# The first projection of a two-block kernel in four quarters of its input dimension, with the modulation weights read in smaller units around it

## The chip, the cores and the metric

The kernel runs on one core of one Trainium2 chip. The core has TensorE (matrix multiply, called PE in the profile; its weight loads are listed as PEld), VectorE (DVE), ScalarE (ACT), GpSimd (POOL) and SyncE (SP), and 16 DMA engines that bring data from HBM. The metric is device time in microseconds (us), lower is better; below, a time "at 68.65" is counted from the start of the span of the profiled execution.

## The reference

Two transformer-like blocks over 256 tokens of width 2048, all in float32. Only the first block's head matters here:

```
mod = silu(c) @ w_ada + b_ada                     # c: 1 x 2048, w_ada: 2048 x 12288 (96 MB)
sh1, sc1, gt1, sh2, sc2, gt2 = split(mod, 6)
h = rmsnorm(x, g) * (1 + sc1) + sh1
proj = h @ w_in[l]                                # 2048 x 3072: xr, gr, xp
xr = causal_dwconv(xr, w_conv, b_conv)            # 4 taps
hr = rg_lru(xr, ...)                              # two gates (small matmuls), sigmoid, exp, scan
y_pool = pool_mixer(xp, w_pool, ls_pool)          # windows of 2, 4, 8, 16, then a small matmul
y = concat(hr * gelu(gr), y_pool) @ w_out         # 2048 x 2048
x = x + gt1 * y                                   # then the FFN with sh2, sc2, gt2
```

So `sc1` and `sh1` are needed before the first product, `gt1` with the second product, the other three for the FFN. The second block has no modulation.

## The kernel before

Weights are streamed once from HBM; the activations stay in SBUF, features on the partitions and the 256 tokens along the free dimension. The weights come as **slabs** of 256 output columns, each slab in four **chunks** of 512 rows of the input dimension K (0.5 MiB each: 4 K-tiles of 128 rows). The stages up to the FFN are IN (12 slabs, 48 chunks) and OUT (8 slabs, 32 chunks).

A chunk goes through a fixed path. SP loads it into one of 8 `raw` buffers (`load`), ScalarE writes its high part (`convert`, L907, `split[..0..]`), VectorE the low part (L1246). TensorE multiplies it in three products (high by high, high by low, low by high) in `multiply`: one matmul of 512 columns against both parts of the activation at once (L556) and one of 256 columns (L563), for each of two column blocks. `split` has 4 buffers, so the convert of chunk G+4 waits until chunk G is multiplied (`chunk_used`). At the end of a slab ScalarE copies the second half of the PSUM result (`copy_low`, L914) and VectorE adds the two halves (`evacuate`, L1259). PSUM holds two slabs, so a slab waits for the evacuation of the slab two before. The last slab of OUT is multiplied by `closing`, in six matmuls of 256 columns for a K-tile (L641 to L643).

IN is done in two halves of K for its first 8 slabs: 16 chunks with the first half of K (blocks 0 to 7 of h), then 16 with the second half, whose sums are added in `evacuate(..., plus=...)`; then slabs 8 to 11 over all of K. So the first product needs only the first half of `sc1` and `sh1`.

The modulation weights are read in 12 **parts** of 1024 columns. Parts 0 to 7 of `ADA_ORDER` are multiplied on TensorE: 8 **pieces** of 1 MiB each (two K-tiles by 1024 columns, rows of 4 KB), four matmuls with one weight column side by side in the array (`multiply_ada`, L584). When a part is done, ScalarE copies its row out of PSUM (`copy_row`, L935), TensorE turns it into columns (`turn_ada`, L592), and VectorE adds the bias (`finish_ada`, L1285). The other four parts are multiplied and added on VectorE, 16 **adds** of 0.5 MiB each (L1299), summed over partitions by `turn_sums` (L604): two parts in OUT, two in the FFN. The lists `RIDE_AT` and `ADD_AT` say behind which chunk each piece or add is used. SP issues all loads from one queue, in order: at step G it issues what is used at chunk G - 8, and waits in front of each load until its buffer is free. Pieces have 4 buffers up to piece 31, and 2 after that (`ada_place`), as the other two become buffers of the gates.

At the start the two first parts (16 pieces) come ahead of the first chunk. The gates (`gates`, `sigmoids`), the recurrence, the windows and the pool products (`pool_product`) of the mixer are placed by hand between the slabs of IN.

## Time and profile before

| | |
|---|---|
| median of 3 runs | 2608.81 us (2608.01 to 2611.77) |
| profiled execution, its own time | 2606.61 us |
| its span | 2604.8 us |
| TensorE, share of the span | 97% |
| VectorE, ScalarE | 68%, 45% |
| DMA, mean over the span | 213 GB/s |
| TensorE clock granted, mean | 0.989 |
| first matmul of IN | at 68.65 us |
| first matmul of OUT | at 279.98 us |
| last matmul of OUT's product | before 389.03 us |

The span is the profiled execution as the core's engines saw it; the own time is 1.8 us more, outside of the span. "Busy" is an average over the whole span: the stages of which this document speaks are its first 389 us.

### The profile page before, as it was taken

How to read it: one execution, taken by the hardware profiler on the slowest of the kernel's cores; microseconds unless marked ns; L12 is line 12 of the kernel's file. 1: busy time of each engine (PE TensorE's matmuls, PEld its weight loads, DVE VectorE, ACT ScalarE, POOL GpSimd, SP SyncE). 2: the span in 40 equal slices, each digit the busy share in tenths (PEclk: the TensorE clock that was granted, in tenths of full speed). 3: DMA queues.
4: the chain of work that ended last, by engine and by line, in shares of the span. 5: the costliest groups of instructions: out<-in, count | busy, mean ns of one | idle time of the engine just before them, and what ended most of it. 6: DMA issues, size and time to landing. Idle time of an engine off the chain costs nothing.

```text
span 2604.8 us, 39862 instructions
## 1 busy us (share of the span) xinstructions
PE 2535.4 (97%) x14572; PEld 2150.0 (83%) x14572; DVE 1781.5 (68%) x2300; ACT 1179.7 (45%) x1439; POOL 10.0 (0%) x37
## 2 busy tenths in 40 slices
PE   4999999999999999999999999999999999999998
PEld 0667688888888888888888888888888888888887
DVE  2468698955555555687686565676788668875886
ACT  1345345444444444563454554445544444444443
POOL 1000000000000000000000000000000000000000
PEclk8999999999999999999999999999999999999999
DMA  9978987955555555565555456566555655555554
GB/s 369 408 263 328 381 335 270 343 180 186 190 188 186 191 188 188 165 193 174 185 170 170 162 170 193 184 189 194 172 184 192 200 187 187 186 191 179 191 167 124
DMA packets 156329, 553.95 MB, mean 213 GB/s; under 512 B 16176, under 2 KB 20272, under 8 KB 156224
## 3 DMA queue, kind: packets, MB, share of 16 engines
q1 hardware_dynamic: 155376, 549.85, 62.0%
q0 software_dynamic: 848, 2.69, 0.3%
q8 instruction: 68, 1.11, 0.2%
q14 instruction: 37, 0.30, 0.0%
HBM read 550.38 MB, written 2.10 MB: 212 GB/s over the span
## 4 chain that ended last, share of the span: by engine, by line
PE 89%; DVE 5%; DMA 3%; ACT 1%; issue 1%; SPq 0%; DVEq 0%; ACTq 0%
PE ps L556 54%; PE ps L563 26%; DMA ride<-in_w_ada 3%; PE ps L553 2%; PE pm L584 2%; DVE split L1246 1%; PE ps L560 1%; DVE acc_out L1299 1%; ACT split L907 1%; DVE x_t L1402 0%; DVE val L1259 0%; PE pm L792 0%; PE pm L705 0%; PE pm L604 0%; DVE val L1375 0%
## 5 line engine op out<-in xcount | busy, mean ns | idle before, releaser
L1246 DVE TENSOR_TENSOR split<-raw,split 128x1024 fp32r<-128x1024 f32 (+1 forms) x864 | 1031.0, 1203 | 696.5 <-ACT split L907 693.4
L907 ACT ACTIVATE split<-raw 128x1024 fp32r<-128x1024 f32 (+1 forms) x864 | 895.9, 1043 | 1145.7 <-PE ps L563 1085.7
L556 PE MATMUL ps<-h_s,split 128*128 128x512 f32 x3880 | 1233.6, 399 | 14.2 <-DVE split L1246 6.6
L563 PEld LDWEIGHTS ps<-h_s,split 128*128 128x128 f32 x3880 | 732.7, 189 | 173.6
L563 PE MATMUL ps<-h_s,split 128*128 128x256 f32 x3880 | 765.7, 279 | 0.0
L556 PE MATMUL ps<-mid_s,split 128*128 128x512 f32 x2336 | 735.1, 396 | 0.5 <-DVE split L1246 0.4
L556 PEld LDWEIGHTS ps<-h_s,split 128*128 128x128 f32 x3880 | 595.3, 190 | 48.4 <-issue 42.8
L563 PEld LDWEIGHTS ps<-mid_s,split 128*128 128x128 f32 x2336 | 438.8, 188 | 103.8
L563 PE MATMUL ps<-mid_s,split 128*128 128x256 f32 x2336 | 458.9, 278 | 0.0
L556 PEld LDWEIGHTS ps<-mid_s,split 128*128 128x128 f32 x2336 | 355.6, 189 | 7.2 <-issue 5.2
L914 ACT ACTIVATE low<-ps 128x512 f32<-128x512 f32 x230 | 133.4, 580 | 0.0
L584 PE MATMUL pm<-ride,c_act 128*1 128x512 f32 x512 | 72.6, 641 | 38.3 <-DMA ride<-in_w_ada 38.3
L1259 DVE TENSOR_TENSOR val<-ps,low 128x512 f32<-128x512 f32 x126 | 86.2, 684 | 1.2 <-ACT low L914 1.1
L1687 DVE SCALAR_TENSOR_TENSOR conv_o<-up_pad,par,conv_o 128x256 f32<-128x256 f32 x176 | 77.5, 482 | 11.4 <-DVE conv_o L1685 5.6
L553 PE MATMUL ps<-split,h_s 128*128 128x512 f32 x256 | 81.1, 398 | 0.0
L1261 DVE TENSOR_TENSOR low<-ps,low 128x512 f32<-128x512 f32 x88 | 60.2, 684 | 0.2
L584 PEld LDWEIGHTS pm<-ride,c_act 128*1 128x1 f32 x512 | 6.8, 81 | 62.5 <-DMA ride<-in_w_ada 36.2
L560 PEld LDWEIGHTS ps<-split,h_s 128*128 128x128 f32 x256 | 48.1, 188 | 11.4
L560 PE MATMUL ps<-split,h_s 128*128 128x256 f32 x256 | 50.3, 278 | 0.0
L1105 ACT ACTIVATE conv_o<-conv_o 128x512 f32<-128x512 f32 x22 | 13.9, 634 | 65.5 <-DVE conv_o L1687 65.5
L553 PEld LDWEIGHTS ps<-split,h_s 128*128 128x128 f32 x256 | 39.0, 189 | 1.7 <-issue 1.7
L556 PE MATMUL ps<-o_m,split 128*128 128x512 f32 x128 | 40.3, 396 | 0.0
(268 smaller groups left out, 1201.9 us busy)
## 6 DMA issues: line engine op xcount, KB each, us to landing
raw<-in_w_in SPq DMA_DIRECT2D x224, 512.0 KB, 3.4
ride<-in_w_ada SPq DMA_DIRECT2D x64, 1024.0 KB, 8.6
raw<-in_w_ffn_down SPq DMA_DIRECT2D x128, 512.0 KB, 3.3
raw<-in_w_ffn_gate SPq DMA_DIRECT2D x88, 512.0 KB, 3.4
raw<-in_w_ffn_up SPq DMA_DIRECT2D x88, 512.0 KB, 4.1
raw<-in_w_ffn_a SPq DMA_DIRECT2D x88, 512.0 KB, 3.8
raw<-in_w_ffn_b SPq DMA_DIRECT2D x88, 512.0 KB, 4.3
raw<-in_w_out SPq DMA_DIRECT2D x64, 512.0 KB, 5.2
```

Source lines behind the costliest of these rows:

```text
L553: pe.matmul(ps[:, s, b, :], acts[:, k0 + k, 0, b * P:(b + 1) * P], split[:, slot, k, :, :].rearrange("p h n -> p (h n)"), start=start, sto ...
L556: pe.matmul(ps[:, s, b, :], split[:, slot, k, 0, b * P:(b + 1) * P], acts[:, k0 + k, :, :].rearrange("p h t -> p (h t)"), start=start, sto ...
L560: mm = pe.matmul(ps[:, s, b, 0:SLAB], acts[:, k0 + k, 1, b * P:(b + 1) * P], split[:, slot, k, 0, :], start=False, stop=stop)
L563: mm = pe.matmul(ps[:, s, b, 0:T], split[:, slot, k, 1, b * P:(b + 1) * P], acts[:, k0 + k, 0, :], start=False, stop=stop)
L584: mm = pe.matmul(pm[2 + n % 2][g:g + 1, :], c_act[:, k:k + 1], src[:, e, 512 * h:512 * h + 512], start=(i == 0), stop=(i == PIECES - 1))
L907: act.activation(split[:, c, 0:kt, 0, :], raw[:, CHUNKS * s + c, 0:kt, :], ACT.Copy).then_inc(hi_ready, 1)
L914: act.activation(low[:, s, :, :], ps[:, s, :, T:2 * T], ACT.Copy).then_inc(low_copied, 1)
L1246: dve.tensor_tensor(split[:, c, 0:kt, 1, :], raw[:, CHUNKS * s + c, 0:kt, :], split[:, c, 0:kt, 0, :].bitcast(F32), ALU.subtract).then_inc ...
L1259: ins = dve.tensor_tensor(dst, ps[:, s, :, 0:T], both, ALU.add)
L1261: own(dve.tensor_tensor(both, ps[:, s, :, 0:T], both, ALU.add))
L1299: dve.scalar_tensor_tensor(out=sums, in0=piece, scalar=c_act[:, k:k + 1], in1=sums, op0=ALU.mult, op1=ALU.add).then_inc(ada_added, 1)
L1687: ins = dve.scalar_tensor_tensor(out=dst, in0=src, scalar=w, in1=dst, op0=ALU.mult, op1=ALU.add)
```

## The change

IN's first 8 slabs are done in four quarters of K, not two halves: 4 passes over 8 slabs, one chunk each (`one_chunk`). Such a chunk is multiplied in six matmuls of 256 columns for a K-tile, all into the same 256 PSUM columns, and is evacuated by itself: in the first pass by a copy on ScalarE, in the other three by an add on VectorE behind the convert of chunk G+4.

`sc1` and `sh1` are read in 8 **units** of 512 columns (4 pieces of 1 MiB, four K-tiles by 512 columns, rows of 2 KB). A quarter of K needs one unit of each. At the start one unit of `sc1` (4 pieces), two chunks and one unit of `sh1` (4 pieces) are loaded ahead of the rest. In each of the first three passes the 8 pieces of the next two units are used, two behind each of chunks 0, 1, 3 and 4 of the pass. The 32 pieces of four later parts are used from chunk 24 to chunk 47, four every three chunks, two of them behind one chunk; 8 pieces of a fifth part, which VectorE added before, follow in OUT behind every third chunk. VectorE's adds in OUT go from 32 to 16; the FFN's 32 adds stay.

The loads of the identity and the gates' weights on POOL wait for chunk 2, that of `w_pool` for chunk 8. Of the convolution, the first tap with the bias is done on ScalarE (`first_tap`), one block at a time. Gates, windows and pool products are placed anew by chunk (`GATES_AT`, `WINDOWS_AT`, `POOL_AT`).

```diff
+LATE_PARTS = (4, 5, 8, 6, 9, 7, 10, 11)
+UNITS, UNIT_PIECES = 2 * CHUNKS, 4
 PIECES = DB // 2
-EARLY = 2
-EARLY_RING = 4
+UNIT_RING = 4
 LATE_RING = 2
-
-
-HALF_SLABS = 8
-HALF_CHUNKS = 2 * HALF_SLABS
-TENSOR_PARTS = 8
-OUT_ADDS = 2 * DB
+TENSOR_PARTS = 5
+IN_RIDES = 4 * PIECES
+ADD_GROUPS = UNITS + TENSOR_PARTS
+GROUPS = UNITS + len(LATE_PARTS)
+OUT_ADDS = 1 * DB
 OUT_ADD_RING, FFN_ADD_RING = 6, 4
 
 
-def _early(G):
-
-    half, r = divmod(G, HALF_CHUNKS)
-    return r // 2, 2 * half + r % 2
+PASS_SLABS = 8
+PASSES = CHUNKS * PASS_SLABS
+EXTRA = PASSES - PASS_SLABS
+
+
+def _group(piece):
+
+
+    if piece < UNITS * UNIT_PIECES:
+        return divmod(piece, UNIT_PIECES)
+    g, i = divmod(piece - UNITS * UNIT_PIECES, PIECES)
+    return UNITS + g, i
 
 
 def _rides():
 
-    at = list(range(HALF_CHUNKS))
-    at += [HALF_CHUNKS + r + r // 4 for r in range((TENSOR_PARTS - 4) * PIECES)]
+    at = [PASS_SLABS * p + c for p in range(CHUNKS - 1) for c in (0, 0, 1, 1, 3, 3, 4, 4)]
+    at += [PASSES - PASS_SLABS + 3 * r // 4 for r in range(IN_RIDES)]
+    at += [CHUNKS * IN_SLABS + 2 + 3 * r for r in range(TENSOR_PARTS * PIECES - IN_RIDES)]
     return at
 
 
 RIDE_AT = _rides()
-LAST_RIDE = {n: RIDE_AT[PIECES * (n - EARLY) + PIECES - 1] for n in range(EARLY, TENSOR_PARTS)}
-ADD_AT = [50 + 26 * j // 32 for j in range(OUT_ADDS)] + [CHUNKS * 22 + j for j in range(2 * DB)]
-LAST_ADD = {n: ADD_AT[DB * (n - TENSOR_PARTS) + DB - 1] for n in range(TENSOR_PARTS, ADA_PARTS)}
-RIDE_SLABS = (LAST_ADD[ADA_PARTS - 1] + 3) // CHUNKS + 1
+LAST_RIDE = {_group(2 * UNIT_PIECES + r)[0]: at for r, at in enumerate(RIDE_AT)}
+ADD_AT = [50 + 26 * j // OUT_ADDS for j in range(OUT_ADDS)] + [CHUNKS * 22 + j for j in range(2 * DB)]
+LAST_ADD = {ADD_GROUPS + j // DB: at for j, at in enumerate(ADD_AT)}
+GATES_AT = (27, 29, 31, 33)
+WINDOWS_AT = (32, 33, 37, 42)
+POOL_AT = (35, 37, 40, 44)
+RIDE_SLABS = (max(LAST_ADD.values()) + 3) // CHUNKS + 1
 
...
-        def load_ada(slot, n, i):
-            part = ADA_ORDER[n]
-            src = dram["w_ada"][2 * i * P:2 * i * P + 2 * P, part * ADA_COLS:(part + 1) * ADA_COLS]
-            sp.dma_start(ada_slot(slot), src.rearrange("(k p) n -> p k n", p=P)).then_inc(ada_loaded[slot], 16)
-
-        for piece in range(EARLY * PIECES):
-            if piece >= EARLY_RING:
-                sp.wait_ge(ada_multiplied, piece - EARLY_RING + 1)
-            load_ada(piece % EARLY_RING, piece // PIECES, piece % PIECES)
-        for G in range(RAW):
-            slab, c = _early(G)
-            load(0, G, dram["w_in"][slab, c])
+        def load_ada(piece):
+            slot, _, free = ada_place(piece)
+            if free > 0:
+                sp.wait_ge(ada_multiplied, free)
+            g, i = _group(piece)
+            if g < UNITS:
+                first = (0 if g % 2 else D) + 512 * (g // 2)
+                src = dram["w_ada"][4 * i * P:4 * i * P + 4 * P, first:first + 512].rearrange("(k p) n -> p k n", p=P)
+                sp.dma_start(ada_slot(slot, 4), src).then_inc(ada_loaded[slot], 16)
+            else:
+                part = late_part(g)
+                src = dram["w_ada"][2 * i * P:2 * i * P + 2 * P, part * ADA_COLS:(part + 1) * ADA_COLS]
+                sp.dma_start(ada_slot(slot, 2), src.rearrange("(k p) n -> p k n", p=P)).then_inc(ada_loaded[slot], 16)
...
+        for piece in range(UNIT_PIECES):
+            load_ada(piece)
+        for G in range(2):
+            load(0, G, dram["w_in"][G, 0])
+        for piece in range(UNIT_PIECES, 2 * UNIT_PIECES):
+            load_ada(piece)
+        for G in range(2, RAW):
+            load(0, G, dram["w_in"][G, 0])
...
+        pool.wait_ge(constants, 3)
+        pool.wait_ge(chunk_used, 2)
         pool.dma_start(ident[:, :], dram["ident"]).then_inc(ident_loaded, 16)
-        pool.dma_start(w_pool[:, :, :, :], dram["w_pool"].rearrange("g (k p) n -> p g k n", p=P)).then_inc(side_loaded, 16)
-
-        pool.wait_ge(constants, 3)
         for w, sb in ((dram["w_rg_a"], rg_a), (dram["w_rg_i"], rg_i)):
             for k in range(2):
                 pool.dma_start(sb[64 * k:64 * k + 64, :, 64 * k:64 * k + 64], w[k].rearrange("h i j -> i h j"))\
                     .then_inc(side_loaded, 16)
+        pool.wait_ge(chunk_used, PASS_SLABS)
+        pool.dma_start(w_pool[:, :, :, :], dram["w_pool"].rearrange("g (k p) n -> p g k n", p=P)).then_inc(side_loaded, 16)
...
+            bank = pm[2 + g % 2]
+            if g < UNITS:
+                src, last = ada_slot(slot, 4), UNIT_PIECES - 1
+                for e in range(4):
+                    mm = pe.matmul(bank[32 * e:32 * e + 1, :], c_act[:, 4 * i + e:4 * i + e + 1], src[:, e, :],
+                                   start=(i == 0), stop=(i == last))
...
-        def half_slab(E, after=None):
-
-            if E >= 2:
-                pe.wait_ge(evacuated, E - 1)
-            for c in range(2):
-                k0 = KT * (2 * (E // HALF_SLABS) + c)
-                if E % HALF_SLABS == 0:
-                    pe.wait_ge(h_ready, k0 + KT)
-                multiply(2 * E + c, (2 * E + c) % RING, E % 2, h_s, k0, KT, c == 0, c == 1)
-                ride_along(2 * E + c)
...
-        for q in range(IN_SLABS):
-            if q < HALF_SLABS:
-                half_slab(HALF_SLABS + q)
-            else:
-                slab(S_IN + q, q % 2, h_s, rides=True)
-            if 1 <= q <= 4:
-                gates(q - 1)
-            if q == 6:
-                pool_product(0)
-            if 8 <= q <= 10:
-                pool_product(q - 7)
...
+        def one_chunk(G):
+
+            c, q = divmod(G, PASS_SLABS)
+            if G >= 2:
+                pe.wait_ge(evacuated, G - 1)
+            pe.wait_ge(lo_ready, G + 1)
+            for k in range(KT):
+                if q == 0:
+                    pe.wait_ge(h_ready, KT * c + k + 1)
+                for part, x in ((0, 0), (0, 1), (1, 0)):
+                    for b in range(2):
+                        mm = pe.matmul(ps[:, G % 2, b, 0:T], split[:, G % RING, k, part, b * P:(b + 1) * P],
+                                       h_s[:, c * KT + k, x, :], start=(k == 0 and part + x == 0),
+                                       stop=(k == KT - 1 and part == 1))
+            mm.then_inc(chunk_used, 1)
+            ride_along(G)
+
+        for G in range(PASSES):
+            one_chunk(G)
+            if G in GATES_AT:
+                gates(GATES_AT.index(G))
+        for q in range(PASS_SLABS, IN_SLABS):
+            def side(c):
+                G = CHUNKS * q + c
+                if G in GATES_AT:
+                    gates(GATES_AT.index(G))
+                if G in POOL_AT:
+                    pool_product(POOL_AT.index(G))
+            slab(S_IN + q, q % 2, h_s, rides=True, after=side)
...
+        def first_tap(blk):
+            act.wait_ge(evacuated, PASSES - PASS_SLABS + blk // 2 + 1)
+            act.activation(xc[:, blk, :], xr_pad[:, blk, PAD:PAD + T], ACT.Identity, bias=col("b_conv", blk),
+                           scale=col("w_conv", PAD * LB + blk)).then_inc(tap_ready, 1)
...
+        for G in range(PASSES):
+            ahead = G + RING
+            convert(ahead // (2 * CHUNKS), ahead // CHUNKS % 2, ahead % CHUNKS)
+            if G < PASS_SLABS:
+                act.wait_ge(chunk_used, G + 1)
+                act.activation(pass_sum(G), ps[:, G % 2, :, 0:T], ACT.Copy).then_inc(evacuated, 1)
+            first_mid(G)
+            if G == 2:
+                act.wait_ge(lam_abs, 1)
+                act.activation(lam_e[:, :], lam_p[:, :], ACT.Exp, scale=-1.0).then_inc(lam_exp, 1)
+            if G >= PASSES - PASS_SLABS:
+                first_tap(G % PASS_SLABS)
+            if G % PASS_SLABS == 6 and G < PASSES - PASS_SLABS:
+                first = KT * (G // PASS_SLABS + 1)
+                act.wait_ge(mod_ready, first // 2 + 2)
+                for b in range(first, first + KT):
+                    norm_block(0, 0, b)
+        for q in range(PASS_SLABS, IN_SLABS):
+            turn(q // 2, q % 2, mid=lambda c: first_mid(CHUNKS * q + c))
...
-        for q in range(IN_SLABS):
-            if q < HALF_SLABS:
-                E, mid = HALF_SLABS + q, first_mid(q)
-                for c in range(2):
-                    half_converts(E, c)
-                    mid(c)
-                evacuate(E, E % 2, partial(q), plus=partial(q))
-                if q < 4:
-                    conv(q)
-                elif q in (5, 7):
-                    windows((q - 5) // 2)
-            else:
-                turn(q // 2, q % 2, val[:, q % 2, :, :], mid=first_mid(q))
...
+        for G in range(PASSES):
+            c, q = divmod(G, PASS_SLABS)
+            ahead = G + RING
+            convert(ahead // (2 * CHUNKS), ahead // CHUNKS % 2, ahead % CHUNKS)
+            if c > 0:
+                dve.wait_ge(chunk_used, G + 1)
+                if G == PASS_SLABS:
+                    dve.wait_ge(evacuated, PASS_SLABS)
+                dve.tensor_tensor(pass_sum(q), ps[:, G % 2, :, 0:T], pass_sum(q), ALU.add).then_inc(evacuated, 1)
+                dve.wait_ge(evacuated, G + 1)
+            first_mid(G)
+            if G == 0:
+                lam_first()
+            if G == 3:
+                lam_terms()
+            first = KT * (c + 1)
+            if c < CHUNKS - 1 and q == 3:
+                dve.wait_ge(mod_ready, first // 2 + 1)
+                modulated_gain(1, "g_norm_mix", first, KT)
+            if c < CHUNKS - 1 and q in (3, 4):
+                for b in range(first + 2 * (q - 3), first + 2 * (q - 3) + 2):
+                    norm_scaled(0, b).then_inc(norm_t, 1)
+            if c < CHUNKS - 1 and q == 6:
+                for b in range(first, first + KT):
+                    norm_low(0, 0, b)
+            if c == CHUNKS - 1:
+                if q == 0:
+                    dve.wait_ge(h_ready, DB)
+                    own(dve.memset(pool_b[:, :, 0:WPAD], 0.0))
+                else:
+                    conv(q - 1)
+        for q in range(PASS_SLABS, IN_SLABS):
+            turn(q // 2, q % 2, val[:, q % 2, :, :], mid=lambda c: first_mid(CHUNKS * q + c))
```

Three places as the instructions stand. First, SyncE's queue at the start of the program, before: `ride` and `ride_2` (printed as `ride_89`) are the pieces' buffers, `raw` the chunks'.

```order
L403 DMA par<-in_params 128x640
L414 DMA x_t<-in_x_fm 128x16x256
L419 DMA ride<-in_w_ada 128x2x1024 x2
...
L409 DMA raw<-in_w_in 128x1024 x8
L419 DMA ride<-in_w_ada 128x2x1024 [waits ada_multiplied]
L409 DMA raw<-in_w_in 128x1024 [waits lo_ready]
```

And after:

```order
L424 DMA par<-in_params 128x640
L435 DMA x_t<-in_x_fm 128x16x256
L445 DMA ride<-in_w_ada 128x4x512 x2
L445 DMA ride_89<-in_w_ada 128x4x512 x2
L430 DMA raw<-in_w_in 128x1024 x2
L445 DMA ride<-in_w_ada 128x4x512 [waits ada_multiplied] x2
L445 DMA ride_89<-in_w_ada 128x4x512 [waits ada_multiplied] x2
L430 DMA raw<-in_w_in 128x1024 x6
L445 DMA ride<-in_w_ada 128x4x512 [waits ada_multiplied] x2
```

Sixteen pieces stood ahead of eight chunks; now it is four pieces, two chunks, four pieces, six chunks.

Second, VectorE in the chunks behind the first 8, before (L1246 the convert, L1259 the evacuation):

```order
L1246 TENSOR_TENSOR split<-raw,split 128x4x256 [waits hi_ready,evacuated]
L1246 TENSOR_TENSOR split<-raw,split 128x4x256 [waits hi_ready]
L1259 TENSOR_TENSOR xr_pad<-ps,low 128x2x256 [waits low_copied]
L1246 TENSOR_TENSOR split<-raw,split 128x4x256 [waits hi_ready,evacuated]
L1246 TENSOR_TENSOR split<-raw,split 128x4x256 [waits hi_ready]
L1259 TENSOR_TENSOR pool_x<-ps,low 128x2x256 [waits low_copied]
```

And after, in the second pass (L1289 the convert, L1605 the add of the chunk's sum):

```order
L1605 TENSOR_TENSOR xr_pad<-ps,xr_pad 128x2x256 [waits evacuated,chunk_used]
L1289 TENSOR_TENSOR split<-raw,split 128x4x256 [waits hi_ready,evacuated]
L1605 TENSOR_TENSOR xr_pad<-ps,xr_pad 128x2x256 [waits chunk_used]
L1289 TENSOR_TENSOR split<-raw,split 128x4x256 [waits hi_ready,evacuated]
L1605 TENSOR_TENSOR xr_pad<-ps,xr_pad 128x2x256 [waits chunk_used]
L1326 TENSOR_TENSOR mod<-pm,par 128x4 [waits ada_turned,evacuated]
```

Every chunk now has an evacuation, where every second had one.

Third, SyncE's queue where the pieces have two buffers, before:

```order
L419 DMA ride<-in_w_ada 128x2x1024 [waits ada_multiplied]
L409 DMA raw<-in_w_in 128x1024 [waits lo_ready] x2
L419 DMA ride<-in_w_ada 128x2x1024 [waits ada_multiplied]
L409 DMA raw<-in_w_in 128x1024 [waits lo_ready]
L419 DMA ride<-in_w_ada 128x2x1024 [waits ada_multiplied]
```

And after, from chunk 24 on:

```order
L449 DMA ride<-in_w_ada 128x2x1024 [waits ada_multiplied] x2
L430 DMA raw<-in_w_in 128x1024 [waits lo_ready]
L449 DMA ride<-in_w_ada 128x2x1024 [waits ada_multiplied]
L430 DMA raw<-in_w_in 128x1024 [waits lo_ready]
L449 DMA ride<-in_w_ada 128x2x1024 [waits ada_multiplied]
L430 DMA raw<-in_w_in 128x1024 [waits lo_ready]
```

Four pieces to five chunks became four to three, two of them next to each other.

## Rows read from the trace of the kernel before

**Rows 1.** The page: its span, and GB/s in 40 slices of 65 us

```profile
span 2604.8 us, 39862 instructions
...
GB/s 369 408 263 328 381 335 270 343 180 186 190 188 186 191 188 188 165 193 174 185 170 170 162 170 193 184 189 194 172 184 192 200 187 187 186 191 179 191 167 124
```

**Rows 2.** Busy time by stage; columns: stretch, its length, each engine's busy us, clock, DMA share, GB/s

```profile
68.60:134.50 65.90, 65.85 (x384) 44.42 (x384) 31.46 (x40) 23.90 (x29) 0.00 (x0) 0.95 1.02 408
...
140.40:280.00 139.60, 138.83 (x809) 99.10 (x809) 96.75 (x144) 66.49 (x100) 0.00 (x0) 0.98 0.81 303
...
280.00:389.00 109.00, 103.46 (x638) 86.92 (x635) 92.49 (x101) 43.54 (x52) 0.00 (x0) 0.98 0.94 365
```

**Rows 3.** Timeline of TensorE at the start: start us, us, instruction, wait

```profile
37.84 1.04 PE L584 MATMUL pm<-ride,c_act 128*1 128x512 f32 x8 [1.51 <-DMA ride<-in_w_ada]
...
40.62 1.89 PE L584 MATMUL pm<-ride,c_act 128*1 128x512 f32 x8
...
59.06 1.04 PE L584 MATMUL pm<-ride,c_act 128*1 128x512 f32 x8 [1.03 <-DMA ride<-in_w_ada]
...
60.82 1.76 PE L592 MATMUL pm<-sel,row 128*128 128x2 f32 x8 [0.72 <-ACT row L935]
...
68.65 1.19 PE L556 MATMUL ps<-h_s,split 128*128 128x512 f32 x2 [6.07 <-DVE split L1246]
```

**Rows 4.** DMA rates: 4 to 14 us, 14 to 16 us, 92 to 128 us

```profile
DMA packets 2258, 3.52 MB, mean 352 GB/s; under 512 B 52, under 2 KB 1849, under 8 KB 2258
...
14.00:16.00 2.00, 0.00 (x0) 0.00 (x0) 0.81 (x2) 1.60 (x3) 0.00 (x0) 1.00 1.01 225
...
DMA packets 3881, 14.71 MB, mean 409 GB/s; under 512 B 297, under 2 KB 297, under 8 KB 3878
```

**Rows 5.** Timeline of TensorE, a chunk between two pieces

```profile
94.09 1.04 PE L584 MATMUL pm<-ride,c_act 128*1 128x512 f32 x8
...
95.06 0.73 PE L556 MATMUL ps<-h_s,split 128*128 128x512 f32 x2
...
98.04 1.04 PE L584 MATMUL pm<-ride,c_act 128*1 128x512 f32 x8
```

**Rows 6.** Timeline of TensorE in OUT: ordinary tiles, then the closing form

```profile
362.64 0.39 PE L563 MATMUL ps<-mid_s,split 128*128 128x256 f32 x2
...
371.69 0.40 PE L563 MATMUL ps<-mid_s,split 128*128 128x256 f32 x2
...
371.92 0.28 PE L641 MATMUL ps<-mid_s,split 128*128 128x256 f32 x1
...
377.32 0.28 PE L641 MATMUL ps<-mid_s,split 128*128 128x256 f32 x1
...
379.74 1.50 PE L604 MATMUL pm<-ones,acc_out 128*128 128x1 f32 x12 [1.90 <-DVE acc_out L1299]
```

**Rows 7.** Groups of TensorE from 140.4 to 280 us: busy us, mean ns, idle

```profile
L705 PE MATMUL pm<-pool_x,w_pool_sb 128*128 128x256 f32 x32 | 7.9, 389 | 0.0
...
L693 PE MATMUL pm<-xc,rg_a 128*128 128x256 f32 x16 | 5.0, 397 | 0.4 <-ACT gate_i L1022 0.4
...
L592 PE MATMUL pm<-sel,row 128*128 128x2 f32 x24 | 3.2, 254 | 0.0
```

**Rows 8.** Timeline of TensorE at the half's turn

```profile
140.39 1.19 PE L556 MATMUL ps<-h_s,split 128*128 128x512 f32 x2 [3.07 <-issue]
...
145.78 1.27 PE L584 MATMUL pm<-ride,c_act 128*1 128x512 f32 x8
```

**Rows 9.** ScalarE and VectorE within a chunk

```profile
94.25 1.06 ACT L907 ACTIVATE split<-raw 128x1024 fp32r<-128x1024 f32 x1 [2.89 <-PE ps L563]
...
96.48 0.68 DVE L1259 TENSOR_TENSOR xr_pad<-ps,low 128x512 f32<-128x512 f32 x1
```

**Rows 10.** The pieces from 134 to 300 us, issue to landing

```profile
DMA to landing us min/median/max: 4.9/7.1/10.2
```

**Rows 11.** Groups of VectorE up to 420 us

```profile
L1299 DVE SCALAR_TENSOR_TENSOR acc_out<-add_out,c_act,acc_out 128x1024 f32<-128x1024 f32 x30 | 38.4, 1280 | 1.1 <-DMA add_out<-in_w_ada 0.5
```

446 lines of the change are left out of this document (200 added, 246 removed).

## The prediction

> **What bounds the kernel now.** I read the page first: the span is 2604.8 us, and up to about 130 us the DMA moves 369 and 408 GB/s, near what it ever reaches; from there to the FFN it moves 263 to 381, and later under 200 [rows 1]. So the question is where DMA or TensorE is last in each stage before the FFN, and I cut the stretch up to 389 us by stages [rows 2]. In the second half of IN and slabs 8 to 11 (140.4 to 280 us) TensorE is busy 138.8 of 139.6 us. In OUT (280 to 389 us) it is busy 103.5 of 109.0, and VectorE 92.5. The one large hole is the start: the first product begins at 68.65 us, behind sixteen pieces, the last of them multiplied at 59.06 [rows 3]. From the FFN on nothing changes; I count that part as it is.
>
> TensorE's own prices. A chunk with one piece behind it takes 98.04 - 94.09 = 3.95 us [rows 5]. A chunk alone: 13 K-tiles from 362.64 to 371.69 are 0.696 us each, 2.785 a chunk [rows 6]. So a piece costs 1.165 us, and a second one directly behind it 0.97 (94.09 to 95.06) [rows 5]; a pair is 2.14. The new form, six matmuls of 256 columns, is what `closing` does: 45 matmuls from 371.92 to 377.32 are 0.12 us each [rows 6], 2.88 a chunk. The pool products cost 7.9 us, the gates 5.0 for half of their matmuls, which overlap with the other half, so about as much, 7.5; a turn costs some 1.0 (24 matmuls in 3.2) [rows 7]; a sum over partitions 2.0 (12 of its 16 matmuls take 1.50) [rows 6].
>
> **The start.** Three things move the first product. POOL's loads (1.64 MB: `w_pool`, gates, identity) leave the head. From 14 to 16 us, where the gates' short rows flow, the rate is 225 GB/s against 409 later [rows 4], so they cost between 1.64/409 = 4.0 and 1.64/225 = 7.3 us; I take 5.5. Second, piece 7, multiplied at 37.84 before [rows 3], is now the last one needed, with two chunks (1.05 MB, 2.6 us at 409) ahead of it. Third, its rows are 2 KB, not 4. Rows of 1 KB (`x_t`, 4 to 14 us) go at 352, those of 4 KB at 409 [rows 4]; with a fixed cost per row this gives 388 for 2 KB, 2.70 us for a piece in place of 2.56, and 1.1 for eight. The bounds are no loss, and that of the 1 KB rows (0.42 us a piece). The Trainium skill, in "DMA: Bandwidth & Descriptors", section Specifications, has transfers from 512 B up at line rate; by that 2 KB rows cost nothing more, and the sum below would be 2.2 us less. The 1 KB rows' 352 GB/s does not agree with it.
>
> Piece 7 is then there at 37.8 - 5.5 + 2.6 + 1.1 = 36.0. Behind it come its product (1.04), the copy and turn, 2.7 from 59.06 + 1.04 to 60.82 + 1.76 [rows 3], and two norm steps, about 1: the chunks are already split. The first product starts at 40.7, 28 us earlier.
>
> **The first pass gives part back, to the DMA.** Before the second pass can start, pieces 8 to 15 and chunks 2 to 11 must land: behind piece 7 come six chunks (7.7 us), eight pieces (21.6), four more chunks (5.1), and POOL's first loads (0.59 MB, 1.4 to 2.6; 2.0). Piece 15 lands at 36.0 + 36.4 = 72.4. Then its product, chunks 5 to 7 (8.6), a turn: 83.1. In that stage the PE waits 1 to 3 us several times, and behind a wait of 3.07 us at 140.39 it ran at the lower of its two clocks (1.2, not 2.4 GHz): the chunk to 145.78 took 5.4 us [rows 8]. The last chunks may pay 1 us of that: second pass at 84.1.
>
> **Passes two and three.** TensorE: 8 chunks 23.0, four pairs 8.6, two turns 2.0: 33.6. DMA: 8 pieces 21.6 and 8 chunks 10.2, 31.8, with `w_pool` in pass two (2.6) 34.4. TensorE also waits for evacuations: behind a chunk's end come the convert on ScalarE, started at 94.25 right behind the chunk, and VectorE's, then the 128x512 add, which ends at 96.48 + 0.68 = 97.16 [rows 9]: 3.06 us after a chunk's end of 94.1, against 2.88 for the chunk between. That is 0.2 us where no piece stands between, some 0.6 a pass. So 34.4 and 34.2; the fourth pass starts at 152.7. The loss of clock at the turn of the halves (5.4 for 2.8, and the 3.07 us wait) goes away [rows 8], but it is inside the stages that I replace, not a separate gain.
>
> **The last 24 chunks of IN** (8 of the fourth pass, 16 of slabs 8 to 11). TensorE: 23.0 + 44.6 for chunks, 35.8 for 32 pieces (8 pairs, 16 single), 4 turns, 7.5 gates, 7.9 pool: 122.8. DMA: eight groups of three chunks and four pieces, 14.1 us each, 113. Between them stand the two buffers: piece n is issued when n - 2 is multiplied, and lands 4.9 us later at best [rows 10]. I follow one group from the product of its first piece, at 0, the second done at 2.3. The third is issued at 0.1 and lands at 5.2 behind a chunk load; TensorE is there at 5.2. The fourth is issued at 2.4, lands at 9.1, TensorE at 9.2. The next first is issued at 6.4, lands at 13.0 and is done at 14.3. Its partner waits for the fourth (10.3) and lands at 15.5, where TensorE is ready at 14.3: 1.2 lost. So 14.3 a group, 114 in all, if gates, pool products and turns (19) all fell into the DMA's lead; 133 if none did; TensorE's 122.8 is the floor. They stand between the groups, where the loads go on behind them, so I take 127, nearer to TensorE's sum. IN ends at 279.7, against 279.98 before: the stage holds 14 more pieces than before, from 42 to 56 behind the first product, and that takes the gain.
>
> **OUT** no longer has 16 of VectorE's adds (1.28 each, 20.5 us [rows 11]) and one sum. TensorE: 28 chunks 78.0, `closing` 11.5, 8 pieces 9.3, a turn 1.0, one sum 2.0: 101.8. VectorE has 92.5 - 20.5 = 72, and DMA 32 chunks, 8 pieces and 16 adds, 33.6 MB or 82 us: both are under it. Before, 109.0 were TensorE's 101.5 by the same prices (6 pieces, 2 sums) and the waits: pieces behind the adds, and 1.90 for the last add [rows 6]. OUT ends at 381.5, not 389.0.
>
> **The sum.** 40.7 (start) + 43.4 + 34.4 + 34.2 + 127 + 101.8 = 381.5, that is 7.5 us less. The profiled execution took 2606.6, so 2599.1; it stands 2.2 below the median of 2608.8, and against the median this is 2601.3. A measurement of this kernel tells about 0.2% (5.2 us) from nothing.
>
> **What is counted at nothing.** None of these has a row of its own. The first tap on ScalarE lies beside its waits for TensorE; uncovered it would cost 8 times 0.5 us. VectorE between chunks 36 and 42 (multiplier, windows, scan) has about 37 us of work in 37; it falls a chunk behind, and `split` is four ahead, so this costs nothing, or one chunk (3 us) if not. The converts of the first chunks and the terms of lambda lie in the DMA's time.
>
> **Rivals.**
> *It all hides* (chance 0.16). For it: before, 26 pieces in 139.6 us cost no more than 0.8 us of idle TensorE [rows 2]. Then the last 24 chunks take 122.8, 2 KB rows are free (2.2), no clock is lost (1), POOL's loads give 7.3 (1.8), and evacuations nothing (1.2): 7.5 + 4.2 + 6.2 = 17.9 less, 2591. Against it: the DMA was busy 0.81 there and would now be near full.
> *The gain is given back in IN* (0.22). The two buffers with paired pieces cost the whole 133, 6 more than I take: 1.5 less than before, 2607. For it: 4.9 us is the best landing, the median is 7.1 [rows 10]. Against: a median with loads queued ahead is not lost time.
> *The clock stays low through the first pass* (0.14), the one that ends slower. With waits between its pieces TensorE is at 1.2 GHz; then a chunk is 5.4 us [rows 8], a piece 1.89 [rows 3], and the pass 43.2 + 15.1 + 3.5 = 62 in place of 43.4: 18.5 lost, 11 slower than before, 2620. It turns the sign at 7.5 lost, some 15 us at the low clock beyond the DMA's own waits. Against it: from 68.65 on the clock averaged 0.95 with all its pieces [rows 2].
> *As forecast* (0.48): 2596 to 2606.
>
> The 8 in 10 range takes in the first two and the near end of the third: 2590 to 2612. By the same cases: faster 0.48 x 0.85 + 0.16 + 0.22 x 0.15 = 0.60, slower 0.12 from the third and 0.02 from the rest: 0.14; the same 0.26.
>
> **What would show it.** In the profile after: first TensorE matmul of IN at 39 to 43; the first evacuation adds of the second pass at 84 to 88; a matmul on `mid_s` at 275 to 285; the end of OUT near 381, with no wait on the adds; matmuls of 256 columns at 0.12 us; waits of TensorE for pieces in the last 24 chunks of 3 to 10 us in all. The prediction is wrong if a chunk of the new form costs more than 3 us, if TensorE waits on evacuations in more than a few chunks, if the granted clock in the first pass is well under 0.9, or if OUT is not shorter.

## The result, and the profile after

The changed kernel takes 2614.1 us (median of 14 runs), the kernel before 2607.5 (14 runs beside them): a ratio of 1.0027, 95% interval 1.0018 to 1.0035. One of the 14 executions of the changed kernel, at 8486 us, is a slow one and counts in neither the ratio nor its interval. The changed kernel is slower by about 7 us, where 7.5 us less was forecast, and it lies outside the range of 2590 to 2612.

The page of the changed kernel, its first line (it answers to [rows 1]):

```profile
span 2612.3 us, 40585 instructions
```

The profiled execution took 2614.05 us by its own time. I cut its head at the prediction's own steps; the windows of the changed kernel (columns: stretch, length, busy time of each engine, granted clock of TensorE, busy share of the DMA, GB/s), against [rows 2]:

```profile
core 0: us, PE busy (x) PEld busy (x) DVE busy (x) ACT busy (x) POOL busy (x), PEclk, DMA share, GB/s
0.00:40.20 40.20, 19.09 (x84) 4.82 (x85) 13.78 (x28) 12.44 (x20) 2.98 (x26) 0.84 1.00 365
40.20:84.10 43.90, 35.73 (x273) 27.76 (x273) 17.30 (x39) 17.19 (x26) 3.45 (x5) 0.95 1.04 378
84.10:119.70 35.60, 33.25 (x272) 26.06 (x273) 17.92 (x27) 12.61 (x17) 0.91 (x1) 1.00 1.04 390
119.70:153.60 33.90, 33.08 (x273) 26.32 (x273) 18.48 (x28) 11.30 (x15) 0.00 (x0) 1.00 0.93 355
153.60:294.30 140.70, 125.10 (x793) 84.81 (x793) 81.07 (x122) 59.30 (x92) 0.00 (x0) 0.96 0.86 318
294.30:397.00 102.70, 102.70 (x647) 84.83 (x643) 74.61 (x84) 44.67 (x54) 0.00 (x0) 1.00 0.86 327
```

The steps forecast 40.7, 43.4, 34.4, 34.2, 127 and 101.8. All but one came within 1.2 us: 40.2, 43.9, 35.6 and 33.9 for the start and the first three passes, and 102.7 for OUT. The fifth, the last 24 chunks of IN, took 140.7. Everything that is wrong with the sum is in that row: TensorE is idle 15.6 us of it, its clock averages 0.96, and the DMA is at 318 GB/s with a busy share of 0.86, while it ran at 390 with 1.04 two rows above. IN ends at 294.3, not at 279.7, and OUT at 397.0, not at 381.5; before, OUT ended at 389.0. From there on both kernels take 2215.

The chain of waits of TensorE in that stretch (engine, line, what ended the wait: us in total, times, longest):

```profile
PE pm L623 <- DMA ride<-in_w_ada: 15.5, 11, 2.2
PE ps L762 <- DVE h_s L1420: 0.8, 1, 0.8
```

So it is the late pieces. The timeline of TensorE shows where two of these waits stand, and what follows the longest (start, duration, line, what it is, in brackets the wait before it):

```profile
227.81 1.16 PE L623 MATMUL pm<-ride,c_act 128*1 128x512 f32 x8 [2.20 <-DMA ride<-in_w_ada]
228.89 1.87 PE L635 MATMUL pm<-sel,row 128*128 128x2 f32 x8
230.62 1.20 PE L588 MATMUL ps<-h_s,split 128*128 128x512 f32 x2
235.78 1.04 PE L623 MATMUL pm<-ride,c_act 128*1 128x512 f32 x8
...
247.57 1.04 PE L623 MATMUL pm<-ride,c_act 128*1 128x512 f32 x8 [1.11 <-DMA ride<-in_w_ada]
253.37 1.04 PE L623 MATMUL pm<-ride,c_act 128*1 128x512 f32 x8 [1.77 <-DMA ride<-in_w_ada]
259.05 1.04 PE L623 MATMUL pm<-ride,c_act 128*1 128x512 f32 x8
```

The wait at 247.57 is that of a pair's second piece, as the prediction had it. The one at 253.37 is that of a single piece behind the next chunk, which by the prediction came in time. And behind the wait of 2.20 us the chunk from 230.62 to 235.78 took 5.16 us instead of 2.8: from 230.62 to 234.6 the granted clock was 0.50, the lower of the two levels. Now the queue of SP in the same stretch, of the same kernel:

```profile
246.53 0.37 SPq L449 DMA_DIRECT2D ride<-in_w_ada  x1
246.94 0.47 SPq L430 DMA_DIRECT2D raw<-in_w_out  x1
248.67 0.37 SPq L449 DMA_DIRECT2D ride<-in_w_ada  x1
249.08 1.10 SPq L430 DMA_DIRECT2D raw<-in_w_out  x1
254.47 6.05 SPq L449 DMA_DIRECT2D ride<-in_w_ada  x2
260.56 0.47 SPq L430 DMA_DIRECT2D raw<-in_w_out  x1
```

SP issues a piece right behind the product that gives its buffer back (245.43 + 1.04, 247.57 + 1.04, 253.37 + 1.04, 259.05 + 1.04; the row at 254.47 holds two issues, the second at about 260.1). Between 250.2 and 254.4, and again up to 260, it issues nothing, the chunk loads behind included, since they stand in the same queue. What it had issued runs out, and the DMA with it (windows of the same kernel; from 262 to 264 it is back at 399 GB/s):

```profile
258.00:260.00 2.00, 2.00 (x15) 0.91 (x13) 0.00 (x0) 0.78 (x1) 0.00 (x0) 1.00 0.88 360
260.00:262.00 2.00, 2.00 (x15) 1.72 (x12) 1.69 (x2) 2.00 (x5) 0.00 (x0) 1.00 0.39 84
```

That gave three readings to be told apart. **A**: the pieces, in pairs through two buffers, starve TensorE. **B**: the DMA's rate is the limit. **C**: TensorE's added work (chunks of six 256-column matmuls, the part moved from VectorE) is what costs.

### The profile page after: what moved, and what is told of

Read it like the earlier page. It is cut to its first block, busy times and chain, and to the rows that moved or that the text cites. A ratio compares the mean times of both kernels' runs of the same rounds, so it can differ in the third digit from the quotient of the medians.

```text
span 2612.3 us, 40585 instructions
## 1 busy us (share of the span) xinstructions
PE 2546.6 (97%) x14916; PEld 2166.9 (83%) x14916; DVE 1761.6 (67%) x2282; ACT 1185.0 (45%) x1445; POOL 10.0 (0%) x37
## 4 chain that ended last, share of the span: by engine, by line
PE 90%; DMA 5%; DVE 3%; ACT 1%; issue 1%; SPq 0%; DVEq 0%; ACTq 0%
PE ps L588 53%; PE ps L595 26%; DMA ride<-in_w_ada 5%; PE ps L585 2%; PE ps L762 2%; PE pm L623 1%; PE ps L592 1%; DVE split L1289 1%; PE pm L616 1%; ACT split L953 1%; PE pm L838 0%; DVE x_t L1442 0%; PE pm L646 0%; DVE h_s L1637 0%; PE ps L683 0%
## 5 line engine op out<-in xcount | busy, mean ns | idle before, releaser
L1289 DVE TENSOR_TENSOR split<-raw,split 128x1024 fp32r<-128x1024 f32 (+1 forms) x864 | 1030.8, 1203 | 748.8 <-ACT split L953 746.0
L588 PE MATMUL ps<-h_s,split 128*128 128x512 f32 x3624 | 1148.4, 398 | 5.2 <-DVE h_s L1420 2.0
L595 PE MATMUL ps<-h_s,split 128*128 128x256 f32 x3624 | 714.1, 278 | 0.0
L959 ACT ACTIVATE low<-ps 128x512 f32<-128x512 f32 x214 | 124.3, 581 | 0.0
L762 PE MATMUL ps<-h_s,split 128*128 128x256 f32 x768 | 101.2, 289 | 3.2 <-DVE h_s L1420 3.1
L616 PE MATMUL pm<-ride,c_act 128*1 128x512 f32 x256 | 37.9, 688 | 27.8 <-DMA ride<-in_w_ada 27.8
L623 PE MATMUL pm<-ride,c_act 128*1 128x512 f32 x320 | 42.4, 603 | 15.6 <-DMA ride<-in_w_ada 15.5
L592 PEld LDWEIGHTS ps<-split,h_s 128*128 128x128 f32 x256 | 48.1, 188 | 11.4
```

What stands on the lines that cost most here:

```text
L588: pe.matmul(ps[:, s, b, :], split[:, slot, k, 0, b * P:(b + 1) * P], acts[:, k0 + k, :, :].rearrange("p h t -> p (h t)"), start=start, sto ...
L592: mm = pe.matmul(ps[:, s, b, 0:SLAB], acts[:, k0 + k, 1, b * P:(b + 1) * P], split[:, slot, k, 0, :], start=False, stop=stop)
L595: mm = pe.matmul(ps[:, s, b, 0:T], split[:, slot, k, 1, b * P:(b + 1) * P], acts[:, k0 + k, 0, :], start=False, stop=stop)
L616: mm = pe.matmul(bank[32 * e:32 * e + 1, :], c_act[:, 4 * i + e:4 * i + e + 1], src[:, e, :], start=(i == 0), stop=(i == last))
L623: mm = pe.matmul(bank[at:at + 1, :], c_act[:, 2 * i + e:2 * i + e + 1], src[:, e, 512 * h:512 * h + 512], start=(i == 0), stop=(i == last))
L762: mm = pe.matmul(ps[:, G % 2, b, 0:T], split[:, G % RING, k, part, b * P:(b + 1) * P], h_s[:, c * KT + k, x, :], start=(k == 0 and part + ...
```

## The experiments

Times are medians; the ratio is to the kernel before, run beside them on the same chip. Differences to the changed kernel's 2614.1 compare runs of different chips, on which the kernel before took 2606.3 to 2607.9. Lines of a kernel's own profile may lie some lines off those of the changed kernel.

### One: 24 pieces in IN, one behind each chunk

```diff
-IN_RIDES = 4 * PIECES
+IN_RIDES = 3 * PIECES
-    at += [PASSES - PASS_SLABS + 3 * r // 4 for r in range(IN_RIDES)]
-    at += [CHUNKS * IN_SLABS + 2 + 3 * r for r in range(TENSOR_PARTS * PIECES - IN_RIDES)]
+    at += [PASSES - PASS_SLABS + r for r in range(IN_RIDES)]
+    at += [CHUNKS * IN_SLABS + 1 + 3 * r // 2 for r in range(TENSOR_PARTS * PIECES - IN_RIDES)]
```

> The changed kernel, with 24 late pieces instead of 32 in the last 24 chunks of IN, one behind each chunk and none in pairs, and the other 16 in OUT, two for three chunks. TensorE's work is the same in all. Theory A (the late pieces, in pairs through two buffers, starve TensorE): a piece has two chunks and a product, some 8 us, between its buffer's release and its need, more than the median landing of 7.2 us, so the waits for pieces in IN fall from 15.5 us to under 3 and the low clock goes with them; the last 24 chunks take 113 to 116 us, OUT 111, the end of OUT comes at 378 to 382 instead of 397, and the time is 2595 to 2600 us. Theory B (the DMA's rate is the limit, 315 GB/s is what this mix of rows gives): the waits move to OUT with the pieces, and the time stays within 0.2% of 2614. Theory C (the changed kernel's extra work on TensorE, the chunk of six 256-column matmuls and the part moved from VectorE, is what costs): the work is unchanged, so 2611 to 2616.

Measured: 2604.5 us, ratio 0.9992 (0.9983 to 1.0001). The waits for pieces fell to 3.8 us in all, 1.3 of them in the last 24 chunks; IN ended at 271.5 and OUT at 387.0. The same products, placed elsewhere, cost 9.6 us less: C does not hold as the main cause. But A had 2595 to 2600, and the upper end is 4.5 us less than measured, so I compared it with the same pieces in pairs.

### Two: the same 24 pieces in pairs

```diff
-    at += [PASSES - PASS_SLABS + r for r in range(IN_RIDES)]
+    at += [PASSES - PASS_SLABS + r // 2 * 2 for r in range(IN_RIDES)]
```

> The same 24 pieces in the last 24 chunks of IN and 16 in OUT, but in IN in pairs behind every second chunk: the same bytes and the same products as with single pieces. Theory A: the pair's second piece can be issued only when the second of the pair before is multiplied, 5.9 us before it is wanted with a transfer ahead of it, so 1 to 2 us are lost for each of 12 pairs: 12 to 22 us longer than with single pieces, 2608 to 2620. Theories B and C: as with single pieces, within 3 us, since neither bytes nor products differ.

Measured: 2601.8 us, 0.9979 (0.9970 to 0.9988). A's expectation (2608 to 2620) fell: pairs cost nothing, with 2.9 us of waits for pieces in all and 1.0 in the stage. What matters is how many pieces the stage holds, not how they stand. The gap to A's figure is elsewhere; VectorE's timeline of this kernel, and behind it the pool product for which it is waited:

```profile
218.20 1.22 DVE L1520 TENSOR_TENSOR a_sq<-gate_r 128x1024 f32<-128x1024 f32 x1
219.45 1.22 DVE L1521 SCALAR_TENSOR_TENSOR lru_t<-a_sq,lru_t 128x1024 f32<-128x1024 f32 x1
220.59 1.22 DVE L1527 TENSOR_TENSOR gate_i<-gate_i,xc 128x1024 f32<-128x1024 f32 x1
221.84 0.88 DVE L1572 SCALAR_TENSOR_TENSOR mid_s<-pm,par,mid_s 128x256 fp32r<-128x256 f32 x2
```
```profile
222.87 3.75 PE L747 MATMUL pm<-pool_x,w_pool_sb 128*128 128x256 f32 x8 [4.74 <-DVE mid_s L1572]
```

Three instructions of the gates, 3.7 us, stand ahead of the short one that TensorE needs; it waits 4.74 us and comes back at the lower clock (3.75 us for what takes 1.99 elsewhere).

### Three: no transfers of late pieces in IN

```diff
+    def dry(piece):
+        return 0 <= piece - UNITS * UNIT_PIECES < IN_RIDES
...
         def load_ada(piece):
+            if dry(piece):
+                return
```
...and `multiply_ada` does not wait for them.

> The changed kernel without the 32 transfers of late pieces in IN: the products are still made, on what stands in the two buffers, so the modulation of four parts is left out of the result; TensorE's work is the same, and the DMA moves 33.6 MB less in the last 24 chunks. Theories A and B: the stage takes TensorE's own sum, 122.8 by the prediction's prices and 127 with chunks of 3.06 us as measured, IN ends at 277 to 281, and the time is 2597 to 2601. Theory C: TensorE's work itself is longer than the prediction summed, the stage stays at 135 or more, 2608 or more.

Measured: 2597.2 us, 0.9963 (0.9950 to 0.9976). The window of the stage in this kernel (OUT behind it took 102.6 us):

```profile
153.50:276.90 123.40, 120.27 (x792) 83.36 (x790) 80.82 (x121) 58.97 (x92) 0.00 (x0) 0.99 0.31 109
```

So without them the stage takes about what the prediction added up for TensorE (122.8). That is in part luck: TensorE is busy 120.3 us of it, and a wait of 3.1 us for VectorE, which the sum didn't have, makes up the rest. The transfers cost the other 17.3 us. C is out. A and B both expect this, since the run takes away the bytes and the waits for buffers together.

### Four: the passes' chunks in the form of before

```diff
-                for part, x in ((0, 0), (0, 1), (1, 0)):
-                    for b in range(2):
-                        mm = pe.matmul(ps[:, G % 2, b, 0:T], split[:, G % RING, k, part, b * P:(b + 1) * P], ...
+                for b in range(2):
+                    pe.matmul(ps[:, G % 2, b, :], split[:, G % RING, k, 0, b * P:(b + 1) * P],
+                              h_s[:, c * KT + k, :, :].rearrange("p h t -> p (h t)"), start=(k == 0), stop=False)
+                for b in range(2):
+                    mm = pe.matmul(ps[:, G % 2, b, 0:T], split[:, G % RING, k, 1, b * P:(b + 1) * P], ...
```

> The changed kernel with the chunks of the four passes in the form of before, four matmuls for a K-tile, two of 512 and two of 256 columns; the product of the high weights with the low half of the activations falls into columns that nobody adds, so it is left out of the result. The price of a chunk goes from 3.06 to 2.79 us. Theory A: the passes that TensorE bounds (two and three) gain 16 times 0.27, 4 us, and the fourth nothing, as its pieces are waited for anyway: 2609 to 2611. Theory C: all 32 chunks give their 0.27 us, 8.6 us or more with what the higher clock gives: 2603 to 2606. Theory B: 2610 to 2614.

Measured: 2611.1 us, 1.0015 (1.0005 to 1.0024): 3.0 less than the changed kernel, and the two intervals overlap. The 2603 to 2606 of C is missed here too. The expectation's 0.27 us a chunk was a misreading, a chunk with the gap at a following piece set against one without. A pair and a chunk, changed kernel, then this one:

```profile
87.14 1.90 PE L616 MATMUL pm<-ride,c_act 128*1 128x512 f32 x16
88.96 3.13 PE L762 MATMUL ps<-h_s,split 128*128 128x256 f32 x24
92.02 1.92 PE L616 MATMUL pm<-ride,c_act 128*1 128x512 f32 x16
```
```profile
86.71 1.90 PE L616 MATMUL pm<-ride,c_act 128*1 128x512 f32 x16
88.53 0.73 PE L761 MATMUL ps<-h_s,split 128*128 128x512 f32 x2
...
91.52 1.04 PE L616 MATMUL pm<-ride,c_act 128*1 128x512 f32 x8
```

From the pair to the end of the chunk it is 4.88 against 4.81 us: 0.07 a chunk, 2.2 for 32. The prediction had 5.02 for such a pair and chunk.

### Five: four buffers, the same schedule

```diff
+    x_room = x_t.rearrange("p (s e m) t -> p s e (m t)", s=2, e=2)
...
     def ada_slot(slot, k):
-        where = ride[:, slot, :, :] if slot < LATE_RING else ride_2[:, slot - LATE_RING, :, :]
+        more = ride_2 if k == 4 else x_room
+        where = ride[:, slot, :, :] if slot < LATE_RING else more[:, slot - LATE_RING, :, :]
...
     def ada_place(piece):
...
+        if piece < first_late + IN_RIDES:
+            return piece % 4, piece // 4 + 1, piece - 4 + 1
...
+            if piece == UNITS * UNIT_PIECES + 2:
+                sp.wait_ge(h_ready, DB)
```

The two added buffers lie where `x_t` stands, so the kernel leaves out the residual that OUT adds, and SP waits once, in front of the first of them, until `h` is ready.

> The changed kernel, schedule and transfers as they are, with four buffers instead of two for the 32 late pieces of the last 24 chunks: the third and fourth lie where x_t stands, whose values are done with in IN and are wanted again as the residual in OUT, so the residual is left out of the result (pieces of w_ada stand in its place). The runs before have shown that pairs as such cost nothing (24 pieces in pairs: 2601.8, 24 single: 2604.5), which theory A did not expect. Theory A2 (the two buffers keep the DMA from using the time in which TensorE does gates, pool products and turns, and they hold the pieces back behind chunk loads, so that the stage is bound by the chain of release, landing and product; the DMA idles meanwhile): with four buffers the waits for pieces fall from 15.5 to under 5 us, the stage takes 124 to 129 us instead of 140.7, and the time is 2598 to 2604. Theory B (rate: four pieces for three chunks want more than the DMA gives, whatever the buffers): the stage stays at 136 to 141 and the time at 2610 to 2614. 46 MB in 140.7 us are 328 GB/s, in 126 us they would be 366, and up to 390 GB/s were seen in the passes.

Measured: 2598.8 us, 0.9968 (0.9956 to 0.9979), 15.3 less than the changed kernel. The stage in this kernel's windows (OUT took 102.6 us again), and TensorE's waits in it:

```profile
153.50:276.10 122.60, 118.98 (x792) 82.36 (x792) 81.02 (x122) 59.27 (x92) 0.00 (x0) 1.00 0.95 373
```
```profile
PE pm L755 <- DVE mid_s L1580: 3.1, 1, 3.1
PE ps L770 <- DVE h_s L1428: 0.8, 1, 0.8
PE pm L631 <- DMA ride<-in_w_ada: 0.4, 1, 0.4
```

The same bytes in 122.6 us, at 373 GB/s: B is out. The waits for pieces are gone (0.4), and the low clock with them. This is A2 of the expectation, which is A without its word on pairs: two buffers are too few for the pieces of this stage. It takes as long as the kernel without the transfers (122.6 us for 123.4).

### Six: VectorE's order mended

The kernel of experiment two, with two lines moved ahead in `first_mid`:

```diff
+            if G - 1 in POOL_AT:
+                pool_low(POOL_AT.index(G - 1))
             if G in (36, 37):
                 multiplier(G - 36)
...
-            if G - 1 in POOL_AT:
-                pool_low(POOL_AT.index(G - 1))
```

> The kernel with 24 pieces in pairs in IN, and in VectorE's order of chunk 36 the subtraction for the first pool product's low half put ahead of the gates' multiplier and input gate (3.7 us), behind which TensorE waited 4.7 us for it. If that wait is what the rest of the stage loses, it falls to 1.1, the low clock behind it goes (3.75 against 1.99 us for the product), IN ends at 265 to 267 instead of 271.3, and the time is 2595 to 2598. If VectorE as a whole is the bound there, the wait comes back at the next product and the time stays at 2600 to 2602.

Measured: 2597.3 us, 0.9958 (0.9945 to 0.9972). It beats both kernels: 17 us less than the changed one, about 10.5 less than before. Windows of the stage and of OUT, and its waits from 153.2 us to the end of OUT:

```profile
153.20:264.80 111.60, 108.98 (x728) 81.14 (x729) 80.66 (x121) 59.45 (x92) 0.00 (x0) 1.00 0.85 326
264.80:379.00 114.20, 112.21 (x708) 86.09 (x707) 74.89 (x85) 45.02 (x53) 0.00 (x0) 1.00 0.93 363
```
```profile
PE pm L623 <- DMA ride<-in_w_ada: 3.1, 4, 1.1
PE pm L747 <- DVE mid_s L1572: 1.1, 1, 1.1
...
```

Of the 3.1 us, 1.1 are in the stage and 2.0 in OUT.

### Seven: the fifth part back on VectorE

```diff
-TENSOR_PARTS = 5
+TENSOR_PARTS = 4
-OUT_ADDS = 1 * DB
+OUT_ADDS = 2 * DB
-    at += [CHUNKS * IN_SLABS + 1 + 3 * r // 2 for r in range(TENSOR_PARTS * PIECES - IN_RIDES)]
+    at += [CHUNKS * IN_SLABS + 5 * r // 4 for r in range(TENSOR_PARTS * PIECES - IN_RIDES)]
```

> The same, with the fifth part back on VectorE: 32 adds in OUT as before the change, and 8 pieces on TensorE in the first 9 chunks of OUT instead of 16 in all. IN as in the kernel with the subtraction first, to 266. If TensorE alone bounds OUT, OUT has 8 products less and one sum over partitions more, 115 - 9.3 + 1.0 = 107, and the time is 2588 to 2592. If the adds bound OUT as before the change (109.0 with waits for pieces and 1.9 for the last add), OUT is 109 to 112 and the time 2590 to 2596.

Measured: 2599.0 us, 0.9968 (0.9957 to 0.9979); both expected ranges are missed. OUT with 8 products less on TensorE is no shorter:

```profile
265.00:379.90 114.90, 108.56 (x650) 89.25 (x650) 92.69 (x101) 43.61 (x52) 0.00 (x0) 0.96 0.93 365
```

There it waits for pieces (4.4 us) and for the last add (1.9), and the clock falls to 0.96. In this schedule moving the part is worth nothing that can be measured, either way. The run also puts its 8 pieces of OUT closer together (behind the first 9 chunks), so it doesn't tell the adds' share of these waits from that of the pieces' places.

### Eight and nine: two edits undone

On the kernel of experiment six. Eight: without `pool.wait_ge(chunk_used, 2)` and `pool.wait_ge(chunk_used, PASS_SLABS)`, so that GpSimd's loads stand at the head again. Nine, with `first_tap` on ScalarE left empty:

```diff
-            dve.wait_ge(tap_ready, blk + 1)
+            own(dve.tensor_scalar(xc[:, blk, :], xr_pad[:, blk, PAD:PAD + T], col("w_conv", PAD * LB + blk),
+                                  col("b_conv", blk), ALU.mult, ALU.add))
```

> The kernel with 24 pieces in IN and the subtraction first (2597.3 us), with GpSimd's loads (identity, gates' weights, w_pool, 1.64 MB) back at the head of the program, where they stood before the change. By the prediction's term the first product comes 5.5 us later (bounds 4.0 and 7.3), at 45.8. In the first pass the DMA is full, and it then has 0.59 MB less to move (1.4 to 2.6 us), in the second 1.05 MB less (2.6 us). So the third pass starts between 0 and 1.5 us later, and the time is 2597 to 2599: moving these loads gave the start 5.5 us, and the two passes behind took most of it back. If the start's gain is kept to the end, the time is 2602 to 2604.

> The same kernel of 2597.3 us, with the convolution's first tap on VectorE instead of ScalarE: eight instructions of 0.5 us move to VectorE in chunks 24 to 32. The prediction costed this at nothing, at 4 us if uncovered. VectorE is busy 36.5 of 56.5 us there and waits between for ScalarE's convert: nothing is expected, 2596 to 2599. If VectorE is in fact the one that is last (its wait for the first pool product, 1.1 us, grows), 2599 to 2602.

Measured: 2596.8 us, 0.9965 (0.9951 to 0.9979), and 2596.8, 0.9964 (0.9950 to 0.9977). Eight, first product and starts of the third and fourth pass:

```profile
47.16 4.37 PE L760 MATMUL ps<-h_s,split 128*128 128x256 f32 x24 [1.48 <-DVE h_s L1418]
...
121.16 3.10 PE L760 MATMUL ps<-h_s,split 128*128 128x256 f32 x24 [0.81 <-DVE h_s L1418]
...
155.01 3.11 PE L760 MATMUL ps<-h_s,split 128*128 128x256 f32 x24 [0.81 <-DVE h_s L1418]
```

The first product is 6.9 us later (the prediction's bounds for these loads were 4.0 and 7.3), the fourth pass only 1.8 (153.2 in experiment six). In its profile OUT's last matmul is still 2.1 us later, but the medians of five runs (2596.8 and 2597.3) don't show that. So an earlier start is not yet an earlier end: the first pass is bound by the DMA (busy share 1.04 in its window above), which has to move those bytes before or behind it. The first tap on ScalarE costs and gives nothing, as the prediction counted it.

### Ten and eleven: 28 and 20 pieces in IN

```diff
-IN_RIDES = 3 * PIECES
+IN_RIDES = 28
-    at += [PASSES - PASS_SLABS + r // 2 * 2 for r in range(IN_RIDES)]
-    at += [CHUNKS * IN_SLABS + 1 + 3 * r // 2 for r in range(TENSOR_PARTS * PIECES - IN_RIDES)]
+    at += [PASSES - PASS_SLABS + 6 * r // 7 for r in range(IN_RIDES)]
+    at += [CHUNKS * IN_SLABS + 1 + 2 * r for r in range(TENSOR_PARTS * PIECES - IN_RIDES)]
```

and 20, with `6 * r // 5` and `5 * r // 4`.

> The same kernel of 2597.3 us, with 28 of the 40 late pieces in the last 24 chunks of IN (seven for six chunks, four times two behind one chunk) and 12 in OUT. A group of six chunks and seven pieces is 7.7 + 17.9 = 25.6 us of the DMA beside 18.4 + 8.0 = 26.4 of TensorE. With 24 pieces the two buffers lost 3.1 us in waits, with 32 they lost 15.5. If the loss starts where the DMA's need passes TensorE's work between the gates and pool products, it is small here, 2 to 5 us: 2597 to 2600. If it grows evenly with each piece added, it is 9: 2601 to 2606.

> The same kernel of 2597.3 us, with 20 pieces in the last 24 chunks of IN and 20 in OUT. IN gets 4.6 us shorter and OUT as much longer on TensorE; the DMA in OUT has 32 chunks, 20 pieces and 16 adds, 46 MB in 119 us. If TensorE bounds both stages with 24 pieces, nothing changes: 2596 to 2599. If the two buffers still cost in IN, up to 3 us come back: 2594 to 2596. If VectorE or the adds' transfers bound, 2599 or more.

Measured: 2603.8 us, 0.9988 (0.9978 to 0.9997), and 2607.5, 1.0002 (0.9992 to 1.0011). With 28 pieces the waits for pieces in the stage are 8.4 us, halfway between 1.1 (24 pieces, experiment six) and 15.5 (32): the loss grows with each piece added from 24 on. The stage with 28:

```profile
154.00:280.60 126.60, 118.10 (x761) 82.72 (x761) 80.98 (x122) 59.27 (x92) 0.00 (x0) 0.99 0.85 317
```

With 20 the loss is in OUT:

```profile
264.50:389.20 124.70, 117.98 (x747) 87.56 (x746) 75.02 (x85) 46.01 (x54) 0.00 (x0) 1.00 0.93 364
```

OUT takes 10.5 us more for 4 pieces more, of which 4.7 are their products, about 1 a turn that moved with them, and 4.6 more waits for pieces (6.6 against 2.0), again through two buffers, now with adds in the same queue.

IN got only 0.4 shorter (111.2), where the expectation had 4.6. It took the prediction's 1.165 for each of four pieces, in pairs or alone. Two chunks with a pair, in experiment six, and two chunks with two single pieces, in this kernel:

```profile
156.25 1.90 PE L623 MATMUL pm<-ride,c_act 128*1 128x512 f32 x16
...
164.02 1.04 PE L623 MATMUL pm<-ride,c_act 128*1 128x512 f32 x8
```
```profile
157.28 3.13 PE L762 MATMUL ps<-h_s,split 128*128 128x256 f32 x24
...
165.35 3.13 PE L762 MATMUL ps<-h_s,split 128*128 128x256 f32 x24
```

The first is 164.02 - 156.25 = 7.77 us, the second 165.35 - 157.28 = 8.07, so a pair is 0.3 us cheaper for TensorE than two single pieces. Twenty-four pieces in pairs against twenty alone is then 4.7 us less for four pieces and 3.6 us more for twelve pairs taken apart. With that, an estimate from the rows closes: 1.1 less for the pieces, 1.0 for the turn and 1.1 for the wait for a piece that is gone, against 0.8 and 0.6 more in waits for VectorE (the first pool product, a gate) and 1.5 for that product at the low clock (3.52 us for 1.97).

## Why the prediction was wrong

**The start.** Right in sum: 40.2 for 40.7. Its term for GpSimd's loads was 5.5, and undoing it measured 6.9, within its bounds; the two norm steps, taken at about 1, are a wait of 1.48 us in the profile.

**The first pass, passes two and three.** Right in sum: 113.4 for 112.0, but in passes two and three by terms that offset each other. A chunk of the new form with a piece behind it takes 3.06 us from start to start (88.96 to 92.02), more than the 3 that the prediction named as a sign of being wrong, where it had 2.88; a pair takes 1.82 where it had 2.14. TensorE waited for no evacuation there (0.6 a pass in the prediction), but 0.8 us for `h` at the head of each pass and once 1.5 for a piece. For the 2 KB rows the trace bears the term out: with a busy share of 1.04 the DMA moved 390 GB/s in pass two, and 394 from 97 to 119 us, behind `w_pool`, for 2 KB and 4 KB rows mixed, while [rows 4] has 409 for 4 KB rows. The Trainium skill, in "DMA: Bandwidth & Descriptors", section Specifications, would have had them at line rate; here the measurement decides against it.

**The last 24 chunks of IN.** This is the step that failed: "They stand between the groups, where the loads go on behind them, so I take 127". It took 140.7, above the upper bound of 133 too. Two things in it were wrong, and both are one mechanism.

First, the landing. The recurrence used 4.9 us, the best of [rows 10], and added the queue only in part; the rival paragraph set the median of 7.1 aside, "a median with loads queued ahead is not lost time". In the changed kernel the median is 7.2. A buffer's turn is then 7.2 from its release to the landing and 1.0 for the product, and in that time the two buffers bring two pieces: an estimate of 16 turns of 8.2, 131 us, for 32 pieces, before anything else stands in the way, and 115 for 28, 98 for 24. The stages took 140.7, 126.6 and 111.6 (118.1 before VectorE's order was mended). TensorE's own busy time is 120.3 with 32 pieces (experiment three), 118.1 with 28 and 109.0 with 24. So at 24 TensorE is last, and at 32 the turn of the buffers is; the 9.5 us between its 131 and 140.7 aren't placed. At 28 the larger of the two doesn't give the stage: the 8.4 us of waits come on top of the busy time. The same estimate fits the kernel before, whose 26 pieces need 13 turns of 8.1, 105 us, beside 138.8 of TensorE.

Second, "the loads go on". They don't: the loads behind a piece stand in SP's queue behind its wait for a buffer. While TensorE does gates, turns and pool products, at most two pieces can come in and the chunks ahead of the next piece, and then the DMA runs dry: 84 GB/s from 260 to 262 us. With four buffers the same loads do go on, at 373 GB/s, and the stage takes 122.6. The Trainium skill, in "Trainium Kernel Development and Optimization", section Best Practices, advises to double-buffer for performance; these rows show two buffers that overlap the transfers and still lose 15.5 us, since their turn of 8.2 us is longer than TensorE's work for two pieces (122.8 / 16 = 7.7 by the prediction's sum).

The 18.1 us between the changed kernel and that with four buffers come out of their rows: waits for pieces 15.5 against 0.4, TensorE busy 125.1 against 119.0 (the low clock), less 3.1 for the pool product that then has to wait for VectorE.

**OUT.** Right, 102.7 for 101.8, against 109.0 before, and its reason stands as far as the rows go. Before, TensorE was busy 103.5 of 109.0 and waited 3.6 for pieces and 1.9 for the last add; after, it waits for nothing. So the gain is in the waits, as the prediction had it, and not in the work. In seven, with the adds back, waits of the same two kinds came back (4.4 and 1.9) and, with the clock at 0.96, took what 8 products less would give; how much of that is the adds' isn't separated there.

**The sum.** 381.5 + 13.7 for the step that failed + 1.8 for the others gives 397.0.

**The rivals.** "The gain is given back in IN" named the right place and the right two buffers, at less than half their price (6 us over the forecast's 127, measured 13.7); its 133 was a bound only with landings of 4.9. "It all hides" had the stage right for a kernel with four buffers (122.8 for 122.6), but not its time (2591 for 2598.8). The clock in the first pass was 0.95, so that rival did not come.

**What was counted at nothing.** The first tap: right. VectorE's 37 us between chunks 36 and 42, "or one chunk (3 us) if not": in the changed kernel it was hidden, because TensorE was late itself. Once TensorE was on time it cost the 4.7 us of experiment two, and the low clock behind it; mending the order took the stage from 118.1 to 111.6 us.

## What to carry to other kernels

When transfers go through a ring, compute its turn (release, queue, landing, use) with the median landing that the trace shows in a loaded stage, not with the best one, and set the number of turns against the length of the whole stage. A queue that waits for a buffer holds back every load behind it, so work that is "between" the pieces is no cover for them. And when a stall is removed, look for the engine that was just behind it: its order can be mended for nothing, and an earlier start counts only if the stage behind it isn't bound by the same transfers.

## What was not expected of the hardware

The lower clock did not follow the longest waits alone. Two more rows of the changed kernel's timeline of TensorE:

```profile
174.44 1.89 PE L623 MATMUL pm<-ride,c_act 128*1 128x512 f32 x8 [1.69 <-DMA ride<-in_w_ada]
...
283.85 1.04 PE L623 MATMUL pm<-ride,c_act 128*1 128x512 f32 x8 [1.82 <-DMA ride<-in_w_ada]
```

Behind 1.69 us (and behind 2.20 at 227.81) the clock was low, behind 1.82 (and 1.77 at 253.37) it was not. The same wait for VectorE in experiment three, and then in five:

```profile
227.07 2.76 PE L755 MATMUL pm<-pool_x,w_pool_sb 128*128 128x256 f32 x8 [3.13 <-DVE mid_s L1580]
```
```profile
228.04 1.97 PE L755 MATMUL pm<-pool_x,w_pool_sb 128*128 128x256 f32 x8 [3.12 <-DVE mid_s L1580]
```

Behind waits of the same length the product ran in part at the low clock in one kernel and at the high clock throughout in the other. What decides it isn't shown here. In the changed kernel's stage the low clock cost some 6 us (TensorE busy 125.1 against 119.0), beside 15.5 of waits.
